# Hybrid decoder step on one core: the expert rows are added to the residual in HBM by the scatter itself, and the last stage reads one row per token

## What is computed

```python
x = x + gate1 * (merged @ w_o)
h = _rmsnorm(x, g_ffn) * (1 + scale2) + shift2
return x + gate2 * _hier_moe(h, ...)      # each token goes to 2 of 32 experts, SwiGLU, FF 256
...
y_prompt = _rmsnorm(xp, g_final)
y_sample = _rmsnorm(xs, g_final)
```

## Time and profile before

| What | Value |
|---|---|
| Median of 3 runs | 789.54 us |
| The profiled execution's own time | 789.53 us |
| Its span, first to last instruction | 787.8 us |
| PE, DVE, ACT, POOL busy | 694.5, 318.0, 165.7, 123.9 us |
| DMA read and written over the span | 198.48 MB, mean 252 GB/s |
| Expert scatters (L829) and gathers (L822) | 32 of each |

### The profile page before, as it was taken

One profiled execution on the slowest core, in us unless ns is written; L12 is line 12 of the kernel. 1 busy time (PEld: TensorE's weight loads), 2 busy tenths in 40 slices (PEclk: granted clock), 3 DMA queues, 4 the chain that ended last, 5 costly groups with the idle time before them and its releaser, 6 DMA issues.

```text
span 787.8 us, 12170 instructions
## 1 busy us (share of the span) xinstructions
PE 694.5 (88%) x5003; PEld 532.7 (68%) x5003; DVE 318.0 (40%) x701; ACT 165.7 (21%) x323; POOL 123.9 (16%) x189
## 2 busy tenths in 40 slices
PE   2589999999999999999999999779999988788820
PEld 1289989879899889999997455555565554455500
DVE  2162232135688773322234765425232322211235
ACT  4062222221154442112110111111111111100001
POOL 2400000410006001000000100123333332222112
PEclk9989999999999999999999999769999999988975
DMA  9843546856143438421105972779999999999873
GB/s 293 331 160 140 215 174 267 324 215 222 54 133 118 151 105 331 169 69 67 55 27 177 415 294 87 255 291 400 415 414 413 411 413 417 416 414 416 356 302 151
DMA packets 40399, 198.48 MB, mean 252 GB/s; under 512 B 8174, under 2 KB 8358, under 8 KB 24720
## 3 DMA queue, kind: packets, MB, share of 16 engines
q1 hardware_dynamic: 31088, 175.42, 57.3%
q0 software_dynamic: 8352, 21.81, 8.0%
q10 hardware_dynamic: 904, 0.47, 0.3%
HBM read 188.54 MB, written 17.40 MB: 261 GB/s over the span
## 4 chain that ended last, share of the span: by engine, by line
PE 81%; DMA 6%; DVE 4%; issue 4%; ACT 2%; SPq 1%; POOL 1%; POOLq 0%; DVEq 0%
PE bank L1632 31%; PE bank L1878 16%; PE bank L1833 7%; PE bank L1900 7%; DMA arena<-in_w_in 5%; PE bank L1776 4%; PE bank L1871 2%; PE bank L1773 2%; PE bank L1570 2%; PE bank L1668 2%; PE bank L1731 1%; PE bank L1794 1%; PE bank L1895 1%; DMA arena<-y_scratch 1%; PE bank L1714 1%
## 5 line engine op out<-in xcount | busy, mean ns | idle before, releaser
L1632 PE MATMUL bank<-h_parts,w_parts 128*128 128x260 f32 x2160 | 273.4, 286 | 0.8 <-DVE w_parts L1068 0.6
L1632 PEld LDWEIGHTS bank<-h_parts,w_parts 128*128 128x128 f32 x2160 | 263.8, 189 | 9.9 <-issue 8.2
L1878 PE MATMUL bank<-arena,arena_b 128*64 128x256 f32 x704 | 89.8, 412 | 13.5 <-issue 9.1
L1068 DVE TENSOR_TENSOR w_parts<-arena,w_parts 128x1024 fp32r<-128x1024 f32 x46 | 56.2, 1222 | 71.3 <-ACT w_parts L897 71.1
L1878 PEld LDWEIGHTS bank<-arena,arena_b 128*64 128x64 f32 x704 | 57.6, 148 | 39.5 <-issue 12.3
L1422 DVE TENSOR_TENSOR arena_b<-bank,arena_b 128x128 f32<-128x128 f32 x32 | 9.3, 292 | 129.8 <-ACT arena_b L1000 129.7
L897 ACT ACTIVATE w_parts<-arena 128x1024 fp32r<-128x1024 f32 x46 | 48.4, 1052 | 55.9 <-DMA arena<-in_w_in 41.9
L829 POOL DMA_INDIRECT y_scratch<-arena_b x32 | 33.2, 1037 | 161.9 <-DVE arena_b L1447 154.4
L1833 PE MATMUL bank<-arena,arena_b 128*128 128x512 f32 x128 | 56.7, 597 | 0.0
L1878 PE MATMUL bank<-arena_b 128*64 128x256 f32 x320 | 40.1, 407 | 6.1 <-issue 5.3
L1900 PE MATMUL bank<-arena,arena_b 128*64 128x512 f32 x176 | 42.3, 593 | 0.8 <-DVE arena_b L1428 0.8
(11 more groups left out here) (301 smaller groups left out, 761.1 us busy)
## 6 DMA issues: line engine op xcount, KB each, us to landing
arena<-in_w_gate_up SPq DMA_DIRECT2D x44, 1024.0 KB, 29.1
arena<-in_w_in SPq DMA_DIRECT2D x46, 512.0 KB, 4.9
arena<-in_w_ada SPq DMA_DIRECT2D x22, 1024.0 KB, 7.2
arena<-in_w_down SPq DMA_DIRECT2D x20, 1024.0 KB
arena_b<-in_w_gate_up SPq DMA_DIRECT2D x20, 1024.0 KB
arena_b<-in_w_down SPq DMA_DIRECT2D x20, 512.0 KB
arena_b<-in_x_prompt SPq DMA_DIRECT2D x8, 512.0 KB, 7.8
arena_b<-q_scratch POOLq DMA_DIRECT2D x3, 1024.0 KB, 5.7
```

The lines of the kernel that those rows point to most:

```text
L1068: dve.tensor_tensor(w_parts[:, n % 2, 1], ring[:, n % WRING], w_parts[:, n % 2, 0], ALU.subtract).then_inc(s_wlo, 1)
L1632: ins = pe.matmul(ps[s][:, 0:HALF], w_parts[:, n % 2, wp, k], h_parts[:, hp, k, s * HALF:(s + 1) * HALF], start=(k == 0 and hp == 1), stop ...
L1878: ins = pe.matmul(ps[2 + b][R * hh:R * hh + R, 0:2 * P], hTe[:, b, c * P + jj * R:c * P + jj * R + R], w_gu[slot][jj][:, c, :, hh * P:(hh ...
```

## The change

The scatter writes no longer to `y_d`, with a place for each of a token's two expert rows, but adds to the residual row in HBM. `x_d` and `y_d` go; `sum_d` (sum_scratch in the views) takes their place, with 1040 half rows: SP writes x there, GpSimd zeros for the 8 samples. The scatter is issued with `compute_op=ALU.add`. It uses the same list as the gather (a token has one place now), and since two experts can have the same token, scatter e first waits until scatter e - 1 has landed. The last stage loads one row per token straight into x, ScalarE squares it with no addition ahead, and the order of blocks and samples on VectorE and POOL is another.

```diff
@@ sync
-                    sp.dma_start(x_d[i * P:i * P + P], x[:, i]).then_inc(s_xw, 16)
+                    sp.dma_start(sums[i * P:i * P + P], x[:, i]).then_inc(s_xw, 16)
...
             sp.wait_ge(s_y, NE - 2)
-            for i in range(4):
-                sp.dma_start(x[:, i], x_d[i * P:i * P + P]).then_inc(s_xl, 16)
             sp.dma_start(gfin_b, g_final.rearrange("(o d) -> o d", o=1).to_broadcast([P, D])).then_inc(s_xl, 16)
...
             for j in range(EUN):
                 sp.wait_ge(s_sc[j], 16 * (NE // EUN))
-            sp.dma_start(yk[:, 0, 0], y4[0:P, 0]).then_inc(s_yfirst, 16)
-            sp.dma_start(yk[:, 0, 1], y4[0:P, 1]).then_inc(s_yk[0], 16)
-            for i in range(1, 4):
-                sp.dma_start(yk[:, i], y4[i * P:(i + 1) * P]).then_inc(s_yk[i], 16)
+            for i in range(4):
+                sp.dma_start(x[:, i], sums[i * P:(i + 1) * P]).then_inc(s_yk[i], 16)
@@ gpsimd
+            pool.dma_start(sums[TP:T].rearrange("b (c s d) -> (b c) s d", c=16, s=2),
+                           past[:, 0].unsqueeze(1).to_broadcast([P, 2, NE])).then_inc(s_zero, 16)
...
             def scatter(e, j):
-                ix = index_of(e, j, 1, si, s_sx)
+                ix = index_of(e, j, 0, si, s_sx)
                 apart(s_ye, e + 1)
-                pool.indirect_dma_start(out=y_d, out_offset=bass.IndirectOffsetOnAxis(ap=ix, axis=0),
-                                        in_=ys[:, j % YB], in_offset=None, bounds_check=last_written, oob_is_err=False
-                                        ).then_inc(s_sc[j], 16)
+                if isinstance(e, int) and e:
+                    pool.wait_ge(s_sc[(e - 1) % EUN], 16 * ((e - 1) // EUN + 1))
+                pool.indirect_dma_start(out=sum_d, out_offset=bass.IndirectOffsetOnAxis(ap=ix, axis=0),
+                                        in_=ys[:, j % YB], in_offset=None, bounds_check=last_row, oob_is_err=False,
+                                        compute_op=ALU.add).then_inc(s_sc[j], 16)
 
             for e in range(EUN):
                 gather(e, e)
+            pool.wait_ge(s_xw, 16 * 5)
+            pool.wait_ge(s_zero, 16)
@@ scalar
             for i in range(3):
-                act.wait_ge(s_x2, 10 + i + 1)
+                act.wait_ge(s_yk[i], 16)
                 act.activation(res[:, i], x[:, i], ACT.Square, scale=1.0 / 32.0, accum_out=ssq[:, i:i + 1]).then_inc(s_sq, 1)
@@ vector
-            first(0)
-            second(0)
-            first(1)
-            mean_square(0, 0)
-            second(1)
-            normed(0, 0)
...
+            mean_square(0)
+            mean_square(1)
+            normed(0)
+            mean_square(2)
+            normed(1)
             samples_summed()
...
+            normed(2)
+            samples_mean_square()
             for c in range(2):
-                normed(4, 3, slice(512 * c, 512 * (c + 1)))
+                normed(3, slice(512 * c, 512 * (c + 1)))
+            samples_normed()
```

More of the change, by code:

```diff
@@ L323, in hybrid_step @@
         mod_d = nc.dram_tensor("mod_scratch", [1 + TS, 6 * D], F32).ap()
-        x_d = nc.dram_tensor("x_scratch", [TP, D], F32).ap()
+        sum_d = nc.dram_tensor("sum_scratch", [2 * T, D // 2], F32).ap()
         xs_d = nc.dram_tensor("xs_scratch", [TS, D], F32).ap()
         h_d = nc.dram_tensor("h_scratch", [2 * T, D // 2], F32).ap()
-        y_d = nc.dram_tensor("y_scratch", [4 * T, D // 2], F32).ap()
         s_x = [sem(f"s_xin{i}") for i in range(5)]
@@ L446, in hybrid_step @@
         s_r64 = sem("s_r64")
-        s_yfirst = sem("s_yfirst")
+        s_zero = sem("s_zero")
         s_xw = sem("s_xw")
@@ L506, in hybrid_step @@
         ys_v = y_sample.rearrange("b o d -> (b o) d")
-        y4 = y_d.rearrange("(t k j) d -> t k (j d)", k=2, j=2)
+        sums = sum_d.rearrange("(t j) d -> t (j d)", j=2)
         def at_least(eng, s, v):
@@ L646, in _ @@
                 sp.dma_start(yp_v[i], res[:, i]).then_inc(s_out, 16)
-            sp.wait_ge(s_res, 4)
-            sp.dma_start(ys_v.rearrange("b (c d) -> (b c) d", c=16), tail_in[:, 0]).then_inc(s_out, 16)
             for c in range(2):
                 half = slice(512 * c, 512 * (c + 1))
-                sp.wait_ge(s_res, 5 + c)
+                sp.wait_ge(s_res, 4 + c)
                 sp.dma_start(yp_v[3][:, half], res[:, 3, half]).then_inc(s_out, 16)
+            sp.wait_ge(s_res, 6)
+            sp.dma_start(ys_v.rearrange("b (c d) -> (b c) d", c=16), tail_in[:, 0]).then_inc(s_out, 16)
             sp.wait_ge(s_out, 16 * 6)
@@ L779, in _ @@
             pool.memset(ones, 1.0)
-            pool.memset(past[:, 0], 0.0)
+            link(pool.memset(past[:, 0], 0.0))
+            pool.dma_start(sums[TP:T].rearrange("b (c s d) -> (b c) s d", c=16, s=2),
+                           past[:, 0].unsqueeze(1).to_broadcast([P, 2, NE])).then_inc(s_zero, 16)
             pool.memset(member[:, 4], 0.0)
@@ L802, in _ @@
             pool.wait_ge(s_h2w[1], 32)
-            last_read, last_written = pool.to_reg(2 * T - 1), pool.to_reg(4 * T - 1)
+            last_row = pool.to_reg(2 * T - 1)
             def apart(s, v):
@@ L855, in _ @@
                 pool.engine_nop().then_inc(s_moe, 2)
-            for n, i in enumerate((0, 1, 4, 2, 3)):
+            for n, i in enumerate((0, 1, 2, 3, 4)):
                 pool.wait_ge(s_ms, 10 + n + 1)
@@ L1023, in _ @@
                 act.wait_ge(s_sc[j], 16 * (NE // EUN))
-            for kk in range(2):
-                act.dma_start(y64[:, kk], y4[TP:T, kk].rearrange("b (c d) -> b c d", c=16)).then_inc(s_yk[4], 16)
+            act.dma_start(y64[:, 0], sums[TP:T].rearrange("b (c d) -> b c d", c=16)).then_inc(s_yk[4], 16)
             for i in range(3):
-                act.wait_ge(s_x2, 10 + i + 1)
+                act.wait_ge(s_yk[i], 16)
                 act.activation(res[:, i], x[:, i], ACT.Square, scale=1.0 / 32.0, accum_out=ssq[:, i:i + 1]).then_inc(s_sq, 1)
@@ L1030, in _ @@
                 half = slice(512 * c, 512 * (c + 1))
-                act.wait_ge(s_x2, 14 + c)
+                if c == 0:
+                    act.wait_ge(s_yk[3], 16)
                 act.activation(res[:, 3, half], x[:, 3, half], ACT.Square, scale=1.0 / 32.0,
@@ L1482, in _, with mean_square, normed @@
                     down_of(o + NE, 0, 16 * o + 16 * (NE // EUN))
[L1484 to L1497, removed]
+            def mean_square(i):
                 dve.wait_ge(s_sq, 15 + i + 1)
                 dve.tensor_scalar(rstd[:, i:i + 1], ssq[:, i:i + 1], EPS, None, ALU.add).then_inc(s_ms, 1)
-            def normed(n, i, c=slice(0, D)):
-                dve.wait_ge(s_rstd, 10 + n + 1)
+            def normed(i, c=slice(0, D)):
+                if i == 0:
+                    dve.wait_ge(s_xl, 16)
+                dve.wait_ge(s_rstd, 10 + i + 1)
                 dve.scalar_tensor_tensor(out=res[:, i, c], in0=x[:, i, c], scalar=rstd[:, i:i + 1], in1=gfin_b[:, c],
@@ L1507, in samples_summed @@
                 dve.wait_ge(s_t64, 48)
-                dve.wait_ge(s_yk[4], 32)
-                link(dve.tensor_tensor(y64[:, 0], y64[:, 0], y64[:, 1], ALU.add))
+                dve.wait_ge(s_yk[4], 16)
                 link(dve.tensor_tensor(y64[:, 0], y64[:, 0], tail_in[:, 1], ALU.mult))
@@ L1519, in samples_normed @@
             def samples_normed():
-                dve.wait_ge(s_rstd, 10 + 3)
+                dve.wait_ge(s_rstd, 10 + 5)
                 dve.scalar_tensor_tensor(out=tail_in[:, 0], in0=tail_in[:, 0], scalar=rstd[:, 4:5], in1=tail_in[:, 2],
                                          op0=ALU.mult, op1=ALU.mult).then_inc(s_res, 1)
-            first(0)
-            second(0)
-            first(1)
-            mean_square(0, 0)
-            second(1)
-            normed(0, 0)
[L1530 to L1533, removed]
-            samples_summed()
[L1535 to L1542, removed]
+            mean_square(0)
[3 more added lines that the diff above has]
+            normed(1)
+            samples_summed()
             dve.wait_ge(s_sq, 20)
             dve.tensor_scalar(rstd[:, 3:4], ssq[:, 3:4], mx[:, 3:4], EPS, ALU.add, ALU.add).then_inc(s_ms, 1)
+            normed(2)
+            samples_mean_square()
             for c in range(2):
-                normed(4, 3, slice(512 * c, 512 * (c + 1)))
+                normed(3, slice(512 * c, 512 * (c + 1)))
+            samples_normed()
         @block.tensor
```

3 lines of the change are left out of this document (1 added, 2 removed).

## The result

The changed kernel takes 822.76 us (median of 4 runs, 820.9 to 824.03) against 789.44 us (also 4 runs): a ratio of 1.0423, 95% interval 1.0407 to 1.0438. It is 33 us slower where the prediction had +14 and 804. The profiled execution took 824.03 us with a span of 822.2 us.

The account below looks back on a forecast made before the run. Full DMA engines bound the expert stage, with PE pacing its first half on weights loaded ahead. The scatter chain costs 24.2 us and the final stage gains 10.1: net +14 on 789.5, forecast 804 us, range 781 to 834.

Parts of the forecast that it names:

- The final stage: After the last landing: eight additions and 2 MB of loads gone, 24.4 to 14.3 us, a gain of 10.1.
- Landing of a plain scatter under load: Expert stage, scatter start to landing: taken as 6.6 us from small POOL writes, bounds 4.4 and 9.6.
- Wake-up: Expert stage, POOL's delay after the awaited landing: taken as 0.5 us, between 0.3 and 0.82.
- What the addition costs a landing: Expert stage, reading the old row in each scatter: taken as 0.9 us, between nothing and 2.35.
- C: Expert stage, cycle per chained scatter: landing, wake-up and addition, 8.0 us, bounds 4.7 and 12.8.
- The drain: End of expert stage: 27.4 scatters out at 757 us, 3.6 left at 6.06 us each, last landing 781.8.
- break-even of 7.0: Expert stage: up to a cycle of 7.0 us the chain costs nothing at the end.
- third rival: Expert stage: the addition is dear, C of 9 to 10 us, giving 822 to 837 us; chance 0.26.
- rival 2: Expert stage, the forecast case: chain with C of 7.5 to 8.6 us, giving 792 to 813 us; chance 0.44.
- The gathers: Expert stage on POOL: gather e + 4 has three experts of slack, so queuing behind the wait does no harm.
- Bytes: Expert stage: additions read 4.0 MB more, up to 9.6 us; last weights at 757 instead of 747.3.
- The reload of x: Drain before 757 us: dropping the 2 MB reload is worth nothing on the path.

Follow-up runs that it names:

- experiment 3: Changed kernel with plain scatters to two places per token, no chain or addition, only the new final stage: 778.69 us, ratio 0.9861 to the kernel before.
- experiment 1: Changed kernel with the addition taken out, each plain scatter still waiting for the one before: 779.97 us, ratio 0.9863 to the kernel before.
- experiment 2: Changed kernel with additions kept, but scatter e waits for e - 4 instead of e - 1: 790.14 us, ratio 1.0012 to the kernel before.
- experiment 8: experiment 1 with the 2 MB load of x put back once expert 29 is done: 782.69 us, ratio 0.9907 to the kernel before.
- experiment 6: Changed kernel with lighter loads, a quarter of gate and up weights from expert 6, half of down weights from expert 7: 750.36 us.

## Why the prediction was off

The mechanism was the forecast one, slower by a chain of landings and eased by a shorter final stage. One term of its sum was clearly too small: what the addition adds to a cycle of the chain. The smaller errors, in the plain chain, the drain and the final stage, are named beside it.

*The final stage.* Forecast 24.4 to 14.3 us, a gain of 10.1. Measured 13.4, a gain of 11.0, and 10.5 alone (experiment 3). Block 1 is scaled by 812.28, 9.3 us after the last landing and not 9.8, and block 2 by 814.26, 11.3 and not 12.3, since the samples' operations between them took 0.7 us in place of 1.2. POOL's first power took 0.57 and not 1.48 us, but that gave little: the scaling behind it stood behind the epsilon of block 1 (809.19) anyway.

*Landing of a plain scatter under load.* Taken as 6.6 from the small writes in the earlier trace rows; the median is 6.8 (experiment 1). *Wake-up:* taken as 0.5, some 0.3 measured. Together that is the 7.1 of the forecast; the mean distance of experiment 1, which is what adds up over the stage, is 7.5, so 0.4 us were missing here.

*What the addition costs a landing: this is the step that failed.* The prediction took 0.9 us, between nothing and 2.35. By the distances of the two chains it is 9.35 - 7.5 = 1.9 us, by the median landings 9.0 - 6.8 = 2.2 with full queues, and 3.74 - 2.35 = 1.4 us with empty ones. POOL's own instruction, with which a landing is counted, is about 0.6 us longer. How the rest divides between the read of the old row and the wait beside the weights, no run here tells. So C was 9.35 and not 8.0: 1.0 us of the 1.35 from the addition, 0.4 from the plain chain. The cost of an operation that no row showed should have been set nearer its upper bound.

*The drain.* Put into the prediction's own sum, 9.35 gives (757 - 538.4) / 9.35 = 23.4 scatters at 757 us, 7.6 left at 6.06 us, 803 + 3 = 806 for the last landing and 828 us in all, against 802.94 and 822.76 measured. The sum lets the last scatters go at PE's 6.06 us; from scatter 24 to 31 they go at (799.20 - 762.18) / 7 = 5.3, the first 4.1 us after the one before, since its rows lay ready, and the last 4.0. In experiment 1 this counts for more: C = 7.5 gives a last landing at 769 by the sum, with the last weights at 747.3, and it came at 758.9. So the break-even of 7.0 was too low. The prediction's third rival (chance 0.26) is the one that came true, but that its 822 us for C = 9 is the measured time to 1 us is luck: at the C that was measured the same sum gives 828. (The upper end of its rival 2 holds a slip: C = 8.6 gives T = 793, not 791.)

*The gathers.* The prediction held that a gather queued behind the chain does no harm, having three experts of slack, and that VectorE's wait would hold up PE. The idle time of PE is put down to the gathers. It changes nothing in the sum, as POOL's wait for the landing before sets the pace in either case.

*Bytes.* Taken as 9.7 us on the last weights, and as mattering little once the chain binds. Both hold: 11.4 us where no chain hides them (experiment 2), and in the changed kernel the weights are there by about 760 us with eight scatters still to come. The rule of the Trainium skill that spoke against the change, on "Collectives: The Full Stack" in the section on the bandwidth ceiling, that an adding transfer reads two sources and goes at half the rate, is stated there for ring collectives. The estimate by it came close: 9.6 us against 11.4 here. The other, the fixed 2 us of "DMA: Bandwidth & Descriptors", section on the anatomy of one SWDGE DMA, agrees here with empty queues alone (2.35 us plain), and not with full ones (6.8).

*The reload of x* was priced at nothing. By the time from scatter 0 to 31 that was right without a chain (217.6 us with it in the kernel before, 217.2 without it in experiment 3), but the same reload costs 2.7 us beside a chain (experiment 8). The changed kernel has no reload and does not pay it.

*Why the chain costs 1.3 us plain and some 33 with the addition.* Up to the pace at which the weights come, a chain only takes away a lead: experiment 1 runs at 7.5 us for an expert in the first half and ends 2 to 3 us later than experiment 3. From scatter 16 to 28, where the weights set the pace, an expert takes 8.5 us in the kernel before (637.11 to 738.86) and 8.6 with additions (experiment 2, 645.20 to 748.64). At 9.35 the chain is the slower one for the whole stage, and the loss grows with each expert until the weights are all in.

## What to carry to other kernels

A wait for the landing of the DMA before turns that DMA's time from issue to landing into a pace. Compare it, in the load that the stage really has, with the pace of the slowest other resource: here a chain at 7.5 us cost 1 to 3 us in all against weights that come at 8.5 (5.5 with the reload of x beside it), and one at 9.35 some 33. Ask first which earlier transfers can touch the same rows at all: here e - 4 was enough, and the distance of 4 took away 33 us. And an addition that is moved into the DMA takes time from the other transfers, so here it is a gain only where the queues have room: -9.7 us with light transfers, none with full ones, where the version with distance 4 ties with the kernel before. No version tried here beats the kernel before with all of its work done.

## What was not expected of the hardware

One and the same adding scatter of 0.125 MB took 3.7 us to land with empty queues, 4.3 at 212 GB/s (experiment 6) and 9.0 at 391 GB/s (the changed kernel, 540 to 640 us); a plain one 2.35 with empty queues and 6.8 at 414 GB/s (experiment 1). And POOL's instruction for an adding indirect DMA takes 1.6 us where the plain one takes 1.0.
